# Expert layers: the result writes move from SyncE's queue to ScalarE's

## What is computed

```
combine = one_hot(expert_id) weighted by weights      # 2 of 16 experts per token
hid = silu(einsum('td,edf->tef', t, w_gate)) * einsum('td,edf->tef', t, w_up)
hid = hid * combine[:, :, None]
out = einsum('tef,efd->td', hid, w_down)              # d = 1024, f = 256
```

## Time and profile before

| | |
|---|---|
| median of three runs | 2450.61 us |
| span of the profiled execution | 2452.2 us (no other time is listed for it) |
| first expert layer, gather of its first rows to its last result gather | about 1639 to 1861 us |
| second expert layer, the same | about 2200 to 2431 us |
| PE, ACT, DVE, POOL busy over the span | 94%, 50%, 52%, 9% |
| result writes | 32, of 512 KB each, all on SyncE's queue |
| DMAs on ScalarE's queue | none |

### The profile page before, as it was taken

One profiled execution on the slowest core, in us unless ns is written; L12 is line 12 of the kernel. 1 busy time (PEld: TensorE's weight loads), 2 busy tenths in 40 slices (PEclk: granted clock), 3 DMA queues, 4 the chain that ended last, 5 costly groups with the idle time before them and its releaser, 6 DMA issues.

```text
span 2452.2 us, 30186 instructions
## 1 busy us (share of the span) xinstructions
PE 2295.1 (94%) x11874; PEld 1103.4 (45%) x11874; DVE 1265.0 (52%) x2492; ACT 1225.2 (50%) x2127; POOL 226.1 (9%) x296
## 2 busy tenths in 40 slices
PE   7989999999999999999999999989996999979995
PEld 3334664444444444444444446543333444543333
DVE  5456656545545546676654594643115644653213
ACT  7543555666556675666665763631115674431112
POOL 0000000000000420000000000011231000011231
PEclk9999999999999999999999999989998999989998
DMA  5220001222222210222212231429983231328996
GB/s 193 86 97 9 1 35 69 104 103 82 95 99 97 104 69 31 91 103 103 82 71 105 104 99 48 200 109 370 397 316 137 100 138 39 156 102 320 398 420 235
DMA packets 68397, 338.24 MB, mean 138 GB/s; under 512 B 12214, under 2 KB 12524, under 8 KB 53900
## 3 DMA queue, kind: packets, MB, share of 16 engines
q1 hardware_dynamic: 50800, 266.10, 28.5%
q0 software_dynamic: 17456, 70.21, 7.5%
HBM read 372.92 MB, written 23.10 MB: 161 GB/s over the span
## 4 chain that ended last, share of the span: by engine, by line
PE 80%; DVE 9%; ACT 5%; DMA 3%; issue 2%; POOL 0%; SPq 0%; DVEq 0%; POOLq 0%; ACTq 0%
PE PB L383 11%; PE PB L388 11%; PE PB L389 11%; PE PB L3194 8%; PE PB L3218 4%; PE PB L1670 3%; PE PB L1671 3%; PE PB L1674 3%; PE PB L408 2%; PE PB L410 2%; PE PB L409 2%; DMA T<-moe_x,small 1%; PE PB L847 1%; PE PB L3181 1%; PE PB L419 1%
## 5 line engine op out<-in xcount | busy, mean ns | idle before, releaser
L388 PE MATMUL PB<-AS,WS 128*128 128x512 f16 x1416 | 537.1, 379 | 16.7 <-ACT AS L478 12.7
L389 PE MATMUL PB<-AS,WS 128*128 128x512 f16 x1416 | 536.7, 379 | 0.0
L383 PE MATMUL PB<-AS,WS 128*128 128x512 f16 x1416 | 508.4, 379 | 2.6 <-DVE AS L1149 2.5
L320 DVE SCALAR_TENSOR_TENSOR WS<-raw,sc,WS 128x1024 f16<-128x1024 f32 (+3 forms) x288 | 324.8, 1188 | 92.2 <-ACT WS L307 92.2
L307 ACT ACTIVATE WS<-raw,sc 128x1024 f16<-128x1024 f32 (+3 forms) x288 | 284.3, 1056 | 64.1 <-DVE sc L287 64.1
L261 ACT ACTIVATE junk<-raw 128x1024 f16<-128x1024 f32 (+3 forms) x288 | 280.5, 974 | 10.4 <-DMA raw<-in_w_out_even 1.4
L3194 PE MATMUL PB<-T 128*64 128x512 f32 x768 | 235.7, 613 | 11.4 <-issue 8.8
L388 PEld LDWEIGHTS PB<-AS,WS 128*128 128x128 f16 x1416 | 138.5, 98 | 196.5 <-ACT AS L478 22.4
L383 PEld LDWEIGHTS PB<-AS,WS 128*128 128x128 f16 x1416 | 138.6, 98 | 172.2 <-DVE AS L1149 4.1
L389 PEld LDWEIGHTS PB<-AS,WS 128*128 128x128 f16 x1416 | 138.6, 98 | 163.1 <-issue 3.4
L3286 ACT ACTIVATE T<-PB 128x256 f32<-128x256 f32 x32 | 12.3, 385 | 288.0 <-PE PB L3194 288.0
(11 more groups left out here) (617 smaller groups left out, 3514.9 us busy)
## 6 DMA issues: line engine op xcount, KB each, us to landing
T<-in_moe_up SPq DMA_DIRECT2D x26, 2048.0 KB, 10.3
raw<-in_w_up SPq DMA_DIRECT2D x22, 2048.0 KB, 7.8
T<-in_moe_down SPq DMA_DIRECT2D x26, 1024.0 KB, 13.0
raw<-in_w_down SPq DMA_DIRECT2D x16, 1408.0 KB, 6.0
raw<-in_w_in_even SPq DMA_DIRECT2D x8, 2048.0 KB, 7.8
raw<-in_w_in_odd SPq DMA_DIRECT2D x8, 2048.0 KB, 7.8
moe_y<-X SPq DMA_DIRECT2D x32, 512.0 KB, 10.2
WS<-in_moe_up SPq DMA_DIRECT2D x6, 2048.0 KB, 15.2
```

What stands on the lines that cost most here:

```text
L320: e.scalar_tensor_tensor(lo[q], raw[q], s, hi[q], MUL, SUB).then_inc(*k.s("dve_split").up("lo", i, q))
L383: return e.matmul(bank, wh[:, q, c, :], act.lo[c], start=False, stop=c == kt - 1)
L388: e.matmul(bank, wh[:, q, c, :], act.hi[c], start=c == 0, stop=False)
L389: e.matmul(bank, wl[:, q, c, :], act.hi[c], start=False, stop=False)
```

## The change

`sp_moe_out` becomes `act_moe_out`, with the same two waits and the same DMA. SyncE no longer calls it. ScalarE calls it for pair b - 2 after the silu of step b, for pair 14 after the loop ahead of the table load, and for pair 15 after the last eviction.

```diff
             for u in range(2):
                 sp_moe_up(k, e, w, layer, n + 2, u)
-        if n > 0:
-            sp_moe_out(k, e, w, layer, n - 1)
-            if n + 1 < NB and experts(n + 1):
-                w.wait_ge(*p.past("down", n - 1))
-                for u in range(2):
-                    sp_moe_down(k, e, w, layer, n + 1, u)
-    sp_moe_out(k, e, w, layer, NB - 1)
+        if n > 0 and n + 1 < NB and experts(n + 1):
+            w.wait_ge(*p.past("down", n - 1))
+            for u in range(2):
+                sp_moe_down(k, e, w, layer, n + 1, u)
     w.wait_ge(*p.past("down", NB - 1))
     sp_load(k, e, w, place(LAST_OUT[layer], 7)[0] + 3)
 
-def sp_moe_out(k, e, w, layer, b):
+def act_moe_out(k, e, w, layer, b):
...
         e.activation(m.sl[b % 2], PB[2 + b % 2][:, 0:256], ACT.Silu).then_inc(*a.up("silu", b))
+        if b > 1:
+            act_moe_out(k, e, w, layer, b - 2)
         if b + 1 < NB:
             turn(b + 1)
         if b > 0:
             down(b - 1)
+    act_moe_out(k, e, w, layer, NB - 2)
     e.preload_act_table_set(ROOT)
     down(NB - 1)
+    act_moe_out(k, e, w, layer, NB - 1)
```

## The result

The changed kernel takes 2461.3 us, the median of seven runs (2457.9 to 2467.8), against 2450.6 us, 10.7 us between the two medians. The ratio on record, which is used from here on, is 1.0040, with a 95% interval of 1.0028 to 1.0051: 9.8 us slower, 6.9 to 12.5. Timed again beside other kernels it was 1.0045 (1.0032 to 1.0058). The forecast was 2455.2 us, on the line between "same" and "slower", with more chance on "same" (0.48) than on "slower" (0.33). The sign was right, the size is about double the forecast +4.6 us. The median lies 0.3 us above the upper end of the range, 2461; by the ratio (2450.6 + 9.8 = 2460.4) it lies just inside.

What follows compares the result with a forecast made beforehand. TensorE sets most steps, DMA bytes the second layer's late ones. First layer 2.0 + 1.0 + 0.3, second 1.25: +4.55 us, on the median's scale 2450.6 + 4.6 = 2455.2 us; 8 in 10 range 2446 to 2461.

Steps and rivals of the forecast that it cites:

- Issue on ACT, evictions, table load: ScalarE in both layers: 0.33 us issues fit in gaps, writes land before evictions need the staging tile, table load unhindered; cost 0.
- Down weights 1.2 us earlier, step 10's wait gone: Second layer: down weights go without the write ahead, so step 10's down product loses its 1.85 us wait, unless bytes bind.
- 512 KB from idle into full time: Second layer: late writes compete with up weights while DMA engines are full; step 15's wait grows 3.85 to 5.1, +1.25 us.
- 0.91 to about 2.5: Sign that the forecast is right: second layer's wait before step 11's up product grows from 0.91 to about 2.5 us.
- The list of waits at the head of the prediction: TensorE's late places: first layer step 11 (2.20 us); second layer steps 11 (0.91), 10 down (1.85), 15 (3.85).
- Step 11 of the first layer: Down weights and write compete with the up gather: wait +2.0 us, and +1.0 us for the up product at lower clock.
- Ends of the layers: First layer's end: last write shares engines with the 2 MB load, landing up to 1.25 us later; +0.3 us (0 to +1.2).
- Nothing moves: Rival: all queues feed the same 16 engines, so order averages out; 2450.6 us, within 1.5 us; chance 0.2.
- Faster: Rival: second layer keeps step 10's saved 1.85 us and later waits shrink; -3.6 to -6.4, middle 2445.6 us; chance 0.25.
- its 0.95: Deciding sign of the faster rival: DMA share in the late windows drops under about 0.95.
- A write holds an eviction: Rival: with three queues a write takes 15 to 20 us and TensorE waits; +10 us, 2460.6; chance 0.1.

Runs made afterwards that it cites:

- e9: Changed kernel, but pair 15's write goes from SP ahead of the 2 MB load and step 10's down weights wait for step 10's up product: 1.0004 (+1.0 us).
- e6: Kernel before, but SP holds the down weights of step 10 until both up gathers of step 11 have landed: 1.0021 (+5.1 us).
- e1: Changed kernel, but the write of pair 15 of each layer is issued by SP again, ahead of the 2 MB load: 1.0027 (+6.6 us).
- e8: Changed kernel, but SP issues the first layer's final 2 MB load only when pair 15's write has landed: 1.0027 (+6.6 us).
- e5: Kernel before, but writes of pairs 0 to 14 go on ACT's queue at their old time, down weights also at their old time: 1.0025 (+6.1 us).

## Why the prediction was right in sign and half the size

- *Issue on ACT, evictions, table load: 0.* Right. The issue costs 0.33 us beside the silu, and no write landed later than 11.8 us.
- *Down weights 1.2 us earlier, step 10's wait gone.* Right: the 1.85 us wait is gone in the changed kernel and in every variant with the write out of the way, and it was spent again at once.
- *512 KB from idle into full time, +1.25 us.* The wait of step 15 grew as it says: 4.83 and 5.11 us, against 3.85 and 4.43 in the two profiles before, +0.8 in the mean. But the second loop lost 3.3 us. **This is the term that was mis-sized, by leaving out step 11 of the second layer.** I had listed its growth only as a sign to look for ("0.91 to about 2.5") and costed it at nothing, since the full engines were to swallow it before step 15. It grew to 5.82 and 5.64, and the up product behind it took 2.7 and 1.5 us longer at the lower clock. The DMA engines did not stay full behind that wait either (0.82 in 2348.50:2360.50, 0.92 in a like window of the second profile, 0.98 or more before). A likely reason is that the next loads wait for the buffers that this up product frees, so that its delay holds them too; no run isolates it. All this was more than the later steps could give back: the wait before step 13 is gone (1.79 and 1.51 us in the two profiles before), but step 15 still starts some 4 us later, counted from the first up product. The list of waits at the head of the prediction leaves out that wait of step 13. e9 shows the cause: hold one pair of down weights by the length of one up product, and the loop is back at 206.9 us, though the late writes stay. That bytes alone set the pace here was thus too simple: the order of the bytes counted for more.
- *Step 11 of the first layer, +2.0, and its clock, +1.0.* Over-sized, as far as two profiles tell. They have waits of 1.75 and 4.03 us, against 2.20 and 1.66; the loop is 1.3 us longer in the mean. The mechanism is the right one (e6 takes the wait away).
- *Ends of the layers, +0.3 us.* **The step that failed.** The reasoning was that two queues take turns, so a write of 512 KB beside a load costs at most 1.25 us more, and that the gathers make it up. It cost 5.0 us of landing and 3.8 us at the end. e1 and e8 show that the load ahead of it does this. The equal sharing came as assumed; what the sum had at nothing is the late start, 4.55 us to the write's first packet where it is 0.83 alone.
- *The rivals.* "Nothing moves" is out by the interval. "Faster" did not come: the 1.85 us came back as a longer wait at step 11. The one late window that fell under its 0.95 (0.82) lies behind that wait. "A write holds an eviction" never happened, though its 2460.6 us was nearest to the measured time: the right number for a reason that no run shows.

The Trainium skill, "DMA: Bandwidth & Descriptors", section "Queues, rings and completion order", has each DMA engine take turns between the queues that have work for it, a packet at a time. An estimate by that rule, from this case's 420 GB/s, is at most 1.25 us more for the last write beside the load. The measured 8.07 against 3.04 us is more: the two queues do alternate, but only from 4.55 us after the write's issue. The same page, "Issuing engines are not separate DMA queues", says that starting DMAs on several engines "will only save the time on the sequencer it takes to initiate the DMA". The trace agrees that all queues share the same bandwidth (about 420 GB/s at the end of the second layer in both kernels), but the time was not unchanged: the move changed which transfer stood in front of which, and that was worth +6.1 us by itself (e5, 2.7 to 9.8).

## What to carry to other kernels

When the DMA engines are full, a transfer that looks like ballast in a queue may be what keeps a large, not yet urgent load behind it from sharing the engines with the urgent one. Before moving it, name for each transfer behind it what it will now compete with and which of the two is needed first; if it is moved, give the less urgent one an explicit wait (here one `wait_ge`, e9). And a small write on which a chain waits should not stand behind a big load, also when they are on different queues: put it ahead of the load in one queue (e1), or hold the load until it has landed (e8).

## What the runs showed of the hardware

- A 512 KB write on ACT's queue, issued 0.78 us after a 2 MB load on SP's, took 8.07, 7.95 and 7.93 us to land, with its first packet 4.4 to 4.6 us after the issue; alone 2.60, with the first packet after 0.83; ahead of the load in one queue 3.04 (2.95 to 3.10 in the other profiles that have it so). What holds it is open; a load of another size ahead of it was not tried.
- ACT starts to issue a DMA while the activation before it in program order is running (0.06 us after its start, with 0.33 us to run), if the DMA's own waits are met.
- Queues with work do not always share evenly. A load and a write that both have rows of 4 KB moved 0.47 MB each (1849.1 to 1851.4 us of the changed kernel). A gather of up weights (16 KB rows) and a write (4 KB rows) moved 0.97 and 0.28 MB (2401 to 2404 us), as in the turns row by row that the prediction assumed.
- TensorE's clock falls or not in the same stretch of the same code from run to run: 10.2 and 14.5 us for the same instructions in two profiles of one kernel. After waits of 3.6 to 6.2 us at step 11, the up product of 7.02 us took 8.54 to 9.86 us in all eight profiles that had such a wait. After shorter waits it went either way: 7.09 us, its usual length in the timeline, after 1.75 and after 2.35 (e1), 8.78 after 1.79 and 2.20.
